# Sampled attention in a hybrid decoder step: odd key/value pages issued from ScalarE's DMA queue

## The reference, cut to what matters

```python
def sample_sparse_attention(q, k_new, v_new, q_idx, kidx_new, w_idx, cache_k, cache_v, cache_kidx,
                            page_table, layer, rel_bias):
    ...
    sc = index_scores(q_idx, w_idx, kidx_all)
    sc = jnp.where(key_pos[None, None, :] <= q_pos[None, :, None], sc, -jnp.inf)
    _, sel = lax.top_k(sc, n_sel)                       # 256 of 2052 positions
    past = jnp.minimum(sel, PAST_LEN - 1)
    phys = jnp.take_along_axis(page_table, (past // PAGE_SIZE).reshape(Bd, -1), axis=1).reshape(sel.shape)
    off = past % PAGE_SIZE
    ...
    k_sel = jnp.where(is_new, take_rows(k_new, new), cache_k[layer, phys, off].astype(k_new.dtype))
    v_sel = jnp.where(is_new, take_rows(v_new, new), cache_v[layer, phys, off].astype(v_new.dtype))
    return sparse_attend(q, k_sel, v_sel, q_pos, sel, rel_bias)
```

## Time and profile before

| what | value |
|---|---|
| median of 3 runs | 3320.12 us (3313.13 to 4272.85) |
| the profiled execution | 3312.37 us |
| its span, first to last instruction | 3310.7 us |
| mean granted TensorE clock in it | 0.908 |
| busy: PE, DVE, ACT, POOL | 89%, 58%, 33%, 8% of the span |
| phase `attend` | from about 1092.7 to 1402 us of the span |
| of it, prompt part | to 1269.75 us |

### The profile page before, as it was taken

How to read it: one execution, slowest core, us unless ns; L and a number is a source line. 1 busy time by engine, 2 the same in 40 slices (tenths; PEclk the granted TensorE clock), 3 DMA queues, 4 the chain that set the end, 5 groups by cost and what they waited for, 6 DMA issues and landing times. The chain is left out here.

```text
span 3310.7 us, 52455 instructions
## 1 busy us (share of the span) xinstructions
PE 2949.3 (89%) x21558; PEld 2652.6 (80%) x21558; DVE 1935.5 (58%) x3399; ACT 1094.9 (33%) x1333; POOL 248.4 (8%) x357
## 2 busy tenths in 40 slices
PE   3999947999985687798999999999999999999995
PEld 2999916878762233497999999999999999999995
DVE  3444336666646763266999989666664444444554
ACT  1222211211112110134444433555554433344441
POOL 0000000000003101100000000232231100000000
PEclk7999957998986557898999999999999999999998
DMA  2444300000015403463555454899998777755551
GB/s 113 152 156 160 112 29 11 17 11 21 11 38 136 153 2 113 146 217 119 182 172 171 168 179 172 307 341 338 332 330 297 286 271 250 253 177 180 182 187 55
DMA packets 145613, 541.86 MB, mean 164 GB/s; under 512 B 25226, under 2 KB 45427, under 8 KB 114387
## 3 DMA queue, kind: packets, MB, share of 16 engines
q1 hardware_dynamic: 110018, 400.11, 35.3%
q0 software_dynamic: 35376, 138.70, 11.9%
HBM read 521.85 MB, written 16.80 MB: 163 GB/s over the span
## 5 line engine op out<-in xcount | busy, mean ns | idle before, releaser
L2393 DVE TENSOR_TENSOR px_w_r<-px_w,px_wh 128x2048 fp32r<-128x2048 f32 x287 | 657.1, 2290 | 461.1 <-ACT px_wh L2050 457.5
L2050 ACT ACTIVATE px_wh<-px_w 128x2048 fp32r<-128x2048 f32 x287 | 549.7, 1915 | 960.6 <-PE px_bank L256 784.9
L254 PE MATMUL px_bank<-pe_high,px_wh 128*128 128x256 f32 (+1 forms) x2560 | 737.1, 288 | 29.2 <-DVE pe_low L2319 14.4
L255 PE MATMUL px_bank<-pe_low,px_wh 128*128 128x256 f32 (+1 forms) x2560 | 733.7, 287 | 0.0
L256 PE MATMUL px_bank<-pe_high,px_w_r 128*128 128x256 f32 (+1 forms) x2560 | 729.3, 285 | 0.0
L254 PEld LDWEIGHTS px_bank<-pe_high,px_wh 128*128 128x128 f32 x2560 | 487.9, 191 | 58.2 <-issue 37.6
L255 PEld LDWEIGHTS px_bank<-pe_low,px_wh 128*128 128x128 f32 x2560 | 486.9, 190 | 0.0
L256 PEld LDWEIGHTS px_bank<-pe_high,px_w_r 128*128 128x128 f32 x2560 | 484.5, 189 | 0.0
L254 PE MATMUL px_pair<-px_arena_gh,px_wh 128*128 128x256 f32 x1024 | 291.5, 285 | 15.5 <-DVE px_arena_gl L2400 15.5
L254 PE MATMUL px_bank<-px_arena_gh,px_wh 128*128 128x256 f32 x1024 | 290.8, 284 | 7.4 <-DVE px_arena_gl L2400 7.2
L255 PE MATMUL px_pair<-px_arena_gl,px_wh 128*128 128x256 f32 x1024 | 290.3, 284 | 0.0
(11 more groups left out here) (469 smaller groups left out, 4688.4 us busy)
## 6 DMA issues: line engine op xcount, KB each, us to landing
px_w<-in_peer_u SPq DMA_DIRECT2D x128, 1024.0 KB, 4.9
px_w<-in_peer_v SPq DMA_DIRECT2D x128, 1024.0 KB, 5.8
in_w<-in_w_in SPq DMA_DIRECT2D x49, 1024.0 KB, 4.9
px_w<-in_peer_wq SPq DMA_DIRECT2D x16, 1024.0 KB, 5.0
px_lay_u_x<-x_rows POOLq DMA_DIRECT2D x32, 512.0 KB, 5.9
px_arena_u_x<-x_rows POOLq DMA_DIRECT2D x32, 512.0 KB, 6.0
px_w<-in_w_o SPq DMA_DIRECT2D x15, 1024.0 KB, 5.0
pq_pages<-in_kv_pages SPq DMA_DIRECT2D x48, 256.0 KB, 6.9
```

The source lines that it names most:

```text
L254: pe.matmul(out, w_high, high, start=start, stop=False, skip_group_check=True)
L255: pe.matmul(out, w_high, low, start=False, stop=False, skip_group_check=True)
L2050: act.activation(w_high[t % 2][:], w[t % SL][:], ACT.Copy).then_inc(raised, 1)
L2393: v.tensor_tensor(w_low[t % SL][:], w[t % SL][:], w_high[t % 2][:], ALU.subtract) \
```

## The change

The odd pages are no longer issued by POOL but by ACT, inside ACT's own list of instructions: the 24 odd pages of samples 0 to 2 ahead of the first exponential of the prompt part; the 8 of sample 3 behind the last exponential of the prompt part; the 16 of samples 4 and 5 in the loop over pairs at i = 1, ahead of that pair's exponential; the 16 of samples 6 and 7 at i = 2. The waits inside `load_pages` are the same as before and are now on ACT. POOL has no instructions left in the phase. The transfers count on four new semaphores of the phase in place of `cx.paged`, and the offset `before` goes away.

```diff
-        pages_in = [[cx.sem(f"as_pages{k}") for k in range(4)], cx.paged]
+        pages_in = [[cx.sem(f"as_pages{q}{k}") for k in range(4)] for q in range(2)]
...
-        before = (0, 16 * B // 2 * PAGES // 4)
...
-            @block.gpsimd
-            def _(pool):
-                load_pages(pool, 1, range(B))
-
...
             @block.scalar
             def _(act):
+                load_pages(act, 1, range(3))
                 for n in range(NCH):
                     for u, (t, hf) in enumerate(units):
                         t0, m = QT_TILES[t]
...
                             .then_inc(exped, 1)
+                load_pages(act, 1, range(3, 4))
                 for i in range(PAIRS):
+                    if 1 <= i and 2 * i + 3 < B:
+                        load_pages(act, 1, range(2 * i + 2, 2 * i + 4))
                     act.wait_ge(s_maxed, 4 * i + 4)
...
-                            pe.wait_ge(pages_in[q][k], before[q] + 16 * PAGES // 2 * ((2 * i + e) // 4 + 1))
+                            pe.wait_ge(pages_in[q][k], 16 * PAGES // 2 * ((2 * i + e) // 4 + 1))
```

## The result

The changed kernel takes 3347.27 us (median of 5 runs, 3339.37 to 3350.16); beside it the kernel before has a median of 3315.93 in 5 runs. The ratio, in which the one run of 4272.85 us is left out, is **1.0092 [1.0073, 1.0111]** (in brackets its 95% interval): slower by nearly 1%, clear of no change, and inside the 2% that the prediction's chances go by. The profiled execution took 3343.75 us with a span of 3342.1, so 31.4 us more span than before.

What follows compares the result with a forecast made beforehand. It took a chain through ACT's exponentials as the bound, delayed by instructions ahead of ready ones. At 1.11 us a page, 56 p - 36.5 gave 25.7 us, added to the 3315.2 mean: 3341 us, range 3328 to 3356.

Steps and rivals of the forecast that it cites:

- The price of a page, 1.11 us by SP's: ACT's issue time per page, taken from SP's first 24 pages: 1.11 us, bounds 0.94 to 1.30.
- the estimate of 3359: All ACT page issues: register loads of about 600 ns add 0.33 us each, 18 us in the sum, giving 3359 us.
- Part 1: Prompt part: 24 pages ahead of the first exponential delay it 23.5 us, 1.7 returns; +21.8 us, bounds +16.5 to +26.4.
- what comes back: First prompt chunk: DVE, done with selection while waiting, starts its reciprocal sooner after the exponential, returning 1.7 us.
- Part 2: Sample 3's 8 pages after the prompt part: 8.9 us of issue, covered with 12 us to spare, costing nothing.
- Part 3: Samples 4 to 7: 16 pages ahead of each exponential of pairs 1 and 2, 15.84 us cover; +1.9 us each, bounds 0 to 4.9.
- The clock's "1.9 us more or less in a pair": A pair's value products: 9.03 or 7.13 us by TensorE's clock level, 1.9 us more or less, inside the range.
- Queues taking turns: Rival: SP and ACT alternate in issuing DMAs, doubling a page to 2.2 us; 87 us slower, 3402 us; chance 5%.
- Slow register load: Rival: each page-number load on ACT takes 482 ns, adding 0.21 us a page, 12 us more, 3353 us; chance 6%.
- A faster prompt part by the pause: Rival: the longer pause puts TensorE's prompt part on its upper clock level, 3315 us or less; chance 4%.
- Hidden: Rival: the issue is hidden after all, requiring the 24 front pages to fit in 4.8 us; chance 1%.
- What is removed: POOL's issue and its 8.5 us drain: nobody waited for them, so DVE and the phase get nothing back.

Runs made afterwards that it cites:

- Experiments 1 and 2: Changed kernel with odd pages partly back on POOL: first those of samples 0 to 2, ratio 1.0026; second those of samples 4 to 7, ratio 1.0055.
- experiment 9: Changed kernel with odd pages of samples 1 and 2 back on POOL, leaving eight ahead of the first exponential; 3329.94 us in one execution.
- experiment 5: Changed kernel with samples 0 to 2's pages in fours at chunk ends, and four pages of samples 4 to 7 moved to SP; 3315.51 us, ratio 0.9999.
- experiment 3: Changed kernel with an unused one-element exponential ahead of the 24 pages, so the table load runs before them; 3343.19 us in one execution.
- 7: Changed kernel with four unused matmuls of 512 columns on PE ahead of each pair's turning; 3332.93 us in one execution.
- Experiment 6: Kernel before, pages on POOL, with an unused copy on ACT ahead of the exponentials of pairs 1 and 2; 3325.04 us in one execution.
- experiment 11: Kernel before with unused matmuls ahead of each pair's turning and, in the prompt part's first six chunks, at chunk ends and before four turnings; 3303.11 us, ratio 0.9964.

## Why the prediction was right, and which terms were off

The forecast was 3341 us in a range of 3328 to 3356, the result 3347.27, and the reason was the right one: the changed kernel loses what stands in front of ready exponentials, not a share of ACT's time. Experiments 1 and 2 show the two places, experiment 9 the price per page, and experiment 5 that the loss goes when the same issues stand elsewhere on ACT's list.

**The price of a page, 1.11 us by SP's.** In steady bursts 1.07. The instruction durations are SP's within 12 ns. The Trainium skill's 600 ns for such a load ("DMA: Bandwidth & Descriptors", section "Latency and other measured facts") are not seen on ACT either (median 279, maximum 468), so the estimate of 3359 that hung on them has fallen.

**Part 1, +21.8.** Measured +23.48. Two errors stand against each other in it: 23 steps at a slightly smaller price brought some 0.8 us less, and the first DMA, 2.76 us in place of 0.35, brought 2.4 more, a cost that the rows of SP and POOL don't show. The table load behind the pages was placed rightly: experiment 3 moves it in front and gets it back. So was what comes back: DVE's reciprocal follows the exponential's start by 0.49 us in place of 2.28, which is 1.79 for the 1.7 predicted, and PE's turning by 1.03 in place of 3.12. From the first chunk's end on (23.35 us late) the chunks have kept their pace, to 0.1 us in all. That they agree so closely is partly luck. The chunks don't have the fixed pace that the prediction gave them: they take 18.9 to 23.1 us, and in both profiled executions one of them is short (19.12 before, 18.93 after, at a granted clock of 0.58). In experiments 3, 6 and 7 none is, and the last seven chunks take 154.1 us in place of 152.1 and 152.3. So the 23.48 could as well have come out 2 us larger or smaller.

**Part 2, nothing.** Measured nothing, with 12 us to spare as predicted.

**Part 3, +1.9 and +1.9.** Measured +1.3 and +1.0 for the late exponentials, 1.5 us less together, mostly by ACT's 1.07 a page.

**The clock's "1.9 us more or less in a pair".** This is the term that was mis-sized. I had it in the range but not in the sum, though the earlier trace rows had the price: value products of 9.03 in one pair and 7.13 in another. What I didn't ask is why they differ, though the trace of before had a hint: PE waited 5.22 us in front of the slow pair's turning and 4.97 in front of each of the others (together the 20.1 of the earlier trace rows). Part 3 lengthens just these waits, to 6.24 and 5.95, and the value products behind them took 2.0 and 2.2 us more; these belonged in the sum. Experiment 6 shows this chain with no page on ACT, and 7 takes it away with the pages still there.

By these terms the sum would have been 23.5 + 2.3 + 4.2 = 30.0 against 25.7, and the range held the rest.

**The rivals.** Queues taking turns: refuted, a page costs ACT 1.07 us and not 2.2, and no DMA on SP is longer (median 333 ns, maximum 422 against 467 before). Slow register load: refuted, its median is 279. A faster prompt part by the pause: not seen, the stretch of the pause itself is at 0.50 and the chunks have their length. Hidden: no, the first exponential was 25 us late. What is removed gave nothing back: POOL's drain is 34 ns in place of 8469 and no one was waiting for it; page landings of the first burst (median 7.8 us, at most 10.3) held nobody. The prediction also took 2% for about the smallest change that a measurement of this kernel tells from none; these runs told 0.9%, and in experiment 11 0.4%.

## What to carry to other kernels

Before moving DMA issues to an engine that looks idle, look not at its busy share but at what becomes ready behind the new place in its list: each issue is sequencer time of about 1.1 us there, and the same issues between two pieces of work that are not yet ready cost nothing. Where a chain's engine waits a little longer in front of PE, price the matmuls behind the wait as well, at both levels of the clock that the trace shows. If two equal groups of one trace differ in duration, ask what stood in front of each before counting either at zero.

## What the runs showed that I had not expected

- ACT's first page DMA took 2.65 to 2.82 us where it opened the phase and was ACT's first DMA, 1.81 behind a table load, 0.36 behind an early DMA, and 0.39 as ACT's first DMA at a later place; the usual one takes 0.345. The cause is open.
- ACT's sequencer issues DMAs while its engine does something else: in experiment 3 it read the first page's number at 1092.4, during the engine's table load (1092.31 to 1093.59), and the exponential of one element ran beside the first page's DMA (1093.56 to 1095.37).
- Waits of 5.2 to 6.4 us in front of PE's turning were followed by value products for which DVE waited 9.7 to 10.2 us, waits of 4.97 by 7.9; with unused matmuls in the wait PE did the turning in 2.3 us in place of 3.9, and turning and products at the upper level.
- Unused matmuls, which are added work for PE, made the whole kernel 0.36% faster (experiment 11), with chunks of 15 us beside one of 26 in one execution.
